# Expert jobs of 128 and of 64 slots in turn, and some weight low parts made by the Pool engine, in the expert stage of a two-layer decoder step

## The reference

```
def _swiglu(h, w_gate, w_up, w_down):
    return (jax.nn.silu(h @ w_gate) * (h @ w_up)) @ w_down

def _moe(h, w_router, b_router, w_gate, w_up, w_down):
    logits = (h @ w_router).astype(jnp.float32) + b_router.astype(jnp.float32)
    top_vals, top_idx = lax.top_k(logits, TOP_K)
    wts = jax.nn.softmax(top_vals, axis=-1)
    combine = jnp.sum(jax.nn.one_hot(top_idx, N_EXPERTS, dtype=jnp.float32) * wts[..., None], axis=-2)
    out = jnp.zeros_like(h)
    for e in range(N_EXPERTS):
        out = out + combine[..., e:e + 1] * _swiglu(h, w_gate[e], w_up[e], w_down[e])
    return out
```

## Time and profile before

| | us |
|---|---|
| median of 3 runs (lowest, highest) | 2112.4 (2107.23, 2112.99) |
| span of the profiled execution | 2107.7 |
| PE busy, share of the span | 2035.7, 97% |
| DVE busy | 1439.6, 68% |
| ACT busy | 1148.5, 54% |
| POOL busy | 130.5, 6% |
| DMA, mean rate over the span | 250 GB/s |

### The profile page before, as it was taken

The page is one execution under the profiler, slowest core; times in us unless marked ns, Lnnn a source line. Parts: engine busy times, 40 slices in busy tenths (PEclk is TensorE's granted clock), DMA queues, the critical chain, the costliest instruction groups (busy, mean ns, idle before and its releaser), DMA issues. The chain is left out here.

```text
span 2107.7 us, 34719 instructions
## 1 busy us (share of the span) xinstructions
PE 2035.7 (97%) x13413; PEld 1830.5 (87%) x13413; DVE 1439.6 (68%) x1595; ACT 1148.5 (54%) x1162; POOL 130.5 (6%) x170
## 2 busy tenths in 40 slices
PE   7999999999999999999999899999999999999997
PEld 5999999888999889989999688888888888888885
DVE  4477445555444455755454699898989898988987
ACT  4433334444333443432443568686868677776865
POOL 3100003200000030000230100000000000000000
PEclk9999999999999999999999999999999999999998
DMA  9634465654766454435654599999999999999996
GB/s 352 213 91 155 129 205 174 203 179 131 219 200 215 136 164 147 122 103 171 184 184 164 189 325 398 327 393 328 380 347 367 358 349 376 326 394 319 403 326 252
DMA packets 244081, 526.67 MB, mean 250 GB/s; under 512 B 18151, under 2 KB 142169, under 8 KB 243970
## 3 DMA queue, kind: packets, MB, share of 16 engines
q1 hardware_dynamic: 234304, 495.78, 67.0%
q0 software_dynamic: 9648, 29.29, 4.5%
q10 hardware_dynamic: 18, 0.04, 0.0%
HBM read 512.44 MB, written 12.59 MB: 249 GB/s over the span
## 5 line engine op out<-in xcount | busy, mean ns | idle before, releaser
L1688 ACT ACTIVATE mhi<-mraw 128x2048 fp32r<-128x2048 f32 (+1 forms) x318 | 574.0, 1819 | 210.5 <-DMA mraw<-in_w_exp_up 72.9
L1157 DVE TENSOR_TENSOR mlo<-mraw,mhi 128x2048 fp32r<-128x2048 f32 (+1 forms) x317 | 677.1, 2163 | 15.7 <-ACT mhi L1688 14.8
L571 DVE TENSOR_TENSOR wlo<-raw,whi 128x1024 fp32r<-128x1024 f32 x244 | 289.1, 1212 | 314.8 <-ACT whi L1397 313.6
L1973 PE MATMUL ps<-h1h,whi 128*128 128x320 f32 x1248 | 385.1, 321 | 8.8 <-DVE h1l L678 3.9
L1974 PE MATMUL ps<-h1l,whi 128*128 128x320 f32 x1248 | 370.7, 309 | 0.0
L2469 PE MATMUL ps<-mhi,xeh 128*128 128x512 f32 (+1 forms) x864 | 326.7, 378 | 1.8 <-DVE xel L1176 1.7
L2470 PE MATMUL ps<-mhi,xel 128*128 128x512 f32 (+1 forms) x864 | 321.3, 372 | 0.0
L1397 ACT ACTIVATE whi<-raw 128x1024 fp32r<-128x1024 f32 x244 | 247.8, 1046 | 118.9 <-PE ps L2358 44.9
L1973 PEld LDWEIGHTS ps<-h1h,whi 128*128 128x128 f32 x1248 | 235.3, 189 | 25.3 <-issue 18.7
L1974 PEld LDWEIGHTS ps<-h1l,whi 128*128 128x128 f32 x1248 | 235.5, 189 | 0.0
L2475 PE MATMUL ps<-mlo,xeh 128*128 128x512 f32 (+1 forms) x864 | 224.5, 371 | 0.0
(11 more groups left out here) (415 smaller groups left out, 2657.1 us busy)
## 6 DMA issues: line engine op xcount, KB each, us to landing
mraw<-in_w_exp_down SPq DMA_DIRECT2D x198, 512.0 KB, 8.6
mraw<-in_w_exp_gate SPq DMA_DIRECT2D x150, 512.0 KB, 5.5
mraw<-in_w_exp_up SPq DMA_DIRECT2D x144, 512.0 KB, 6.5
raw<-in_w_in SPq DMA_DIRECT2D x128, 512.0 KB, 3.9
raw<-in_w_ada SPq DMA_DIRECT2D x64, 512.0 KB, 3.8
mraw<-in_w_exp_gate SPq DMA_DIRECT2D x72, 384.0 KB, 3.6
mraw<-in_w_exp_up SPq DMA_DIRECT2D x72, 384.0 KB, 4.6
pause<-in_w_ada SPq DMA_DIRECT2D x32, 512.0 KB, 6.8
```

Source lines behind the costliest of these rows:

```text
L571: V.tensor_tensor(WLO[:, u % RAW_UNITS, 0:w], RAW[:, u % RAW_UNITS, 0:w], WHI[:, h % HI_UNITS, 0:w].bitcast(F32), ALU.subtract).then_inc(l ...
L1157: V.tensor_tensor(MLO[:, n % RAW_RING, 0:w], MRAW[:, n % RAW_RING, 0:w], MHI[:, n % HI_RING, 0:w].bitcast(F32), ALU.subtract).then_inc(m_l ...
L1688: A.activation(MHI[:, n % HI_RING, 0:w], MRAW[:, n % RAW_RING, 0:w], ACT.Copy).then_inc(m_hi, 1)
L1973: M.matmul(out_, w, v[0], start=start, stop=False, skip_group_check=True)
```

## The change

Only the expert stage changes, in three ways.

Jobs of 64 slots. Expert 0 stays job 0. The other seven are ranked by their number of tokens: the three largest become jobs 2, 4 and 6, the four smallest jobs 1, 3, 5 and 7. Jobs 0, 2, 4, 6 have 128 slots as before ("full" here), jobs 1, 3, 5, 7 have 64 ("half"), and so have extra jobs, of which there are up to six and each takes the next 64 tokens of an expert that has more than its slots. In a half job the stationary operand holds the 64 tokens' high parts in columns 0 to 63 and their low parts in columns 64 to 127 (`XEH`, and `GTH` in the down part), so lines 2470 and 2507 fall away: 8 matmuls a pair for 12. The halves of the result, in rows 0 to 63 and 64 to 127, are added in the `turn`: ACT copies the gate and up sums (`SG`, `SU`), TensorE multiplies each 128 x 128 block of both with `FOLD` (two unit matrices of 64 on each other) in place of one transpose, ACT takes the silu, DVE multiplies (`SGT`), and one pair later ACT and DVE split the product (`half_high`, `half_low`).

Pool makes the low parts of pairs 6, 11, 16, 21, 26 and 31 of jobs 0 to 6, and DVE leaves these out. Jobs 7 and later keep all 35 on DVE. Pool's fetch for the next job stands in its program between pair 16 and pair 21.

Order and tables. The ranking and the half jobs' tables make DVE's small table work in job 0 longer (nine pieces for five, from pair 2 on for pair 17), SP waits for `routed` after job 0's pairs and loads each job's expert number from `XI`, and job 7 has moved into the loop of extra jobs.

```diff
-EXTRA = 4
+HALF = 64
+MAIN = NE - 1
+EXTRA = 6
 JOBS = NE + EXTRA
+TURNS = 6
 HI_RING, RAW_RING = 5, 7
+POOL_PAIRS = (6, 11, 16, 21, 26, 31)
+DVE_PAIRS = PAIRS - len(POOL_PAIRS)
...
-TABLE_PAIRS = {17: 0, 20: 1, 22: 2, 25: 3, 28: 4}
+TABLE_PAIRS = {2: 0, 4: 1, 6: 2, 8: 3, 17: 4, 19: 5, 21: 6, 23: 7, 25: 8}
...
-            with sp.Fori(1, NE) as job:
-                load_job(job, job)
             sp.wait_ge(sem("routed"), 1)
-            extra = sp.value_load(XI[0:1, 4:5], min_val=0, max_val=EXTRA)
-            with sp.Fori(0, EXTRA) as k:
+            with sp.Fori(0, MAIN // 2) as two:
+                for job in (two * 2 + 1, two * 2 + 2):
+                    e = sp.value_load(XI[0:1, bass.ds(job, 1)], min_val=0, max_val=NE - 1)
+                    load_job(job, e)
+            extra = sp.value_load(XI[0:1, 15:16], min_val=1, max_val=1 + EXTRA)
+            with sp.Fori(0, 1 + EXTRA) as k:
                 with sp.If(k < extra):
-                    e = sp.value_load(XI[0:1, bass.ds(k, 1)], min_val=0, max_val=NE - 1)
-                    load_job(k + NE, e)
+                    e = sp.value_load(XI[0:1, bass.ds(k + MAIN, 1)], min_val=0, max_val=NE - 1)
+                    load_job(k + MAIN, e)
...
+                src, s = PS[:, FILL_BANKS[k], :].rearrange("p (k n) -> p k n", k=4), slice(4 * k, 4 * k + 4)
+                if half:
+                    V.tensor_tensor(XEH[:, s, HALF:P], src[:, :, HALF:P], XEH[:, s, 0:HALF].bitcast(F32),
+                                    ALU.subtract).then_inc(xe_out, 1)
+                else:
+                    V.tensor_tensor(XEL[:, s, :], src, XEH[:, s, :].bitcast(F32), ALU.subtract).then_inc(xe_out, 1)
...
+                (half_constants, ranks, main_slots, main_weights, blocks, owners, extra_slots, extra_weights,
+                 table_out)[part]()
+            def ranks():
+
+
+                n = [P, NE, NE]
+                st(V.tensor_tensor(OH[:, 0], KEY[:, 0:1, :].broadcast_to(n), KEY[:, 0, :].unsqueeze(2).broadcast_to(n),
+                                   ALU.is_gt))
+                st(V.tensor_reduce(KEY[:, 1, :], OH[:, 0], AX.X, ALU.add))
+                st(V.tensor_scalar(KEY[:, 2, :], KEY[:, 1, :], 3.5, None, ALU.is_gt))
+                st(V.tensor_scalar(KEY[:, 3, :], KEY[:, 2, :], 7.0, None, ALU.mult))
+                st(V.scalar_tensor_tensor(KEY[:, 3, :], KEY[:, 1, :], 2.0, KEY[:, 3, :], ALU.mult, ALU.subtract))
+                st(V.tensor_tensor(OH[:, 1], KEY[:, 3:4, :].broadcast_to(n),
+                                   CF[:, C_IOTA8:C_IOTA8 + NE].unsqueeze(2).broadcast_to(n), ALU.is_equal))
+
...
+            def half_low(job, number, k):
+
+
+                f0, nf = tile_at(k)
+                dve.wait_ge(gt_hi, job * TURNS + (k + 1))
+                V.tensor_tensor(GTH[:, f0:f0 + nf, HALF:P],
+                                SGT[:, k % 2, 0:nf * HALF].rearrange("p (k n) -> p k n", k=nf),
+                                GTH[:, f0:f0 + nf, 0:HALF].bitcast(F32), ALU.subtract).then_inc(half_lo, 1)
+
+            def job_dve(job, half, half_next, number=None, first=False, shared=True):
                 m_lo_part(job, 2)
...
                     if p == 0:
                         dve.wait_ge(sem("iw_made"), 1)
...
+                        for k in TURN_PAIRS[p - 1]:
+                            half_low(job, number, k)
                     for s, what, k in SIDE[p]:
...
+                                .then_inc(m_aux_out, 1)
+                        elif what == "turn" and half:
+                            n = tile_at(k)[1] * HALF
+                            dve.wait_ge(gate_out, job * TURNS + (k + 1))
+                            V.tensor_tensor(SGT[:, k % 2, 0:n], SGT[:, k % 2, 0:n], PS[:, bank, 256:256 + n], ALU.mult)\
...
-            with dve.Fori(1, NE) as job:
-                job_dve(job)
+            job_dve(0, False, True, first=True)
+            with dve.Fori(0, MAIN // 2) as two:
+                job_dve(two * 2 + 1, True, False, two)
+                job_dve(two * 2 + 2, False, True)
...
-            with dve.Fori(0, EXTRA) as k:
+            with dve.Fori(0, 1 + EXTRA) as k:
                 with dve.If(k < extra):
-                    job_dve(k + NE)
...
+            def half_high(job, k, s):
+
+
+                f0, nf = tile_at(k)
+                act.wait_ge(m_aux_out, job * JAUX + (AHEAD + s + 1))
+                A.activation(GTH[:, f0:f0 + nf, 0:HALF],
+                             SGT[:, k % 2, 0:nf * HALF].rearrange("p (k n) -> p k n", k=nf), ACT.Copy).then_inc(gt_hi, 1)
...
                 for p in range(PAIRS):
-                    if p < GPAIRS and p % KD == KD - 1:
+                    if half and p < GPAIRS and p % KD == KD - 1:
+                        g, w = p // KD, GROUPS[p // KD][1]
+                        for i in range(2):
+                            act.wait_ge(m_tile, job * 9 + (3 * g + 1 + 2 * i))
+                            A.activation(SG[:, i, 0:w], PS[:, GROUP_BANKS[g][2 * i], 0:w], ACT.Copy)
+                            if i == 0:
+                                act.wait_ge(m_tile, job * 9 + (3 * g + 2))
+                            else:
+                                act.wait_ge(m_used, job * PAIRS + (p + 1))
...
-                        if what == "turn":
+                        if what == "turn" and half:
+                            n = tile_at(k)[1] * HALF
+                            act.wait_ge(m_aux_in, job * JAUX + (s + 1))
+                            if k >= 2:
+                                act.wait_ge(half_lo, number * TURNS + (k - 1))
+                            A.activation(SGT[:, k % 2, 0:n], PS[:, 4 + s % 2, 0:n], ACT.Silu).then_inc(gate_out, 1)
+                        elif what == "turn":
...
+            def job_pool(job):
+
+                for i, n in enumerate(POOL_PAIRS):
+                    if i == len(POOL_PAIRS) // 2:
+                        gather(job + 1)
+                    w = 4 * GROUPS[n // KD][1] if n < GPAIRS else 2 * D
+                    pool.wait_ge(m_hi, job * PAIRS + (n + 1))
+                    pool.tensor_tensor(MLO[:, n % RAW_RING, 0:w], MRAW[:, n % RAW_RING, 0:w],
+                                       MHI[:, n % HI_RING, 0:w].bitcast(F32), ALU.subtract).then_inc(m_lo_pool, 1)
+
...
                 def lo_ready(p):
-                    pe.wait_ge(m_lo, job * PAIRS + (p + 1))
+                    if alone is not None:
+                        pe.wait_ge(m_lo, alone * PAIRS + (MAIN * DVE_PAIRS + p + 1))
+                    elif p in POOL_PAIRS:
+                        pe.wait_ge(m_lo_pool, job * len(POOL_PAIRS) + (POOL_PAIRS.index(p) + 1))
+                    else:
+                        pe.wait_ge(m_lo, job * DVE_PAIRS + (lows_ahead(p) + 1))
...
-                            M.matmul(o_, XEL[:, k, :], hi_[:, s], start=False, stop=False)
+                            if not half:
+                                M.matmul(o_, XEL[:, k, :], hi_[:, s], start=False, stop=False)
...
+                            if kf in TURNED and half:
+                                pe.wait_ge(half_lo, number * TURNS + (TURN_OF[kf] + 1))
+                            elif kf in TURNED:
...
-                            for m in range(tile_at(k)[1]):
+                            for m in range(tile_at(k)[1] if half else 0):
+                                for j, raw in enumerate((SG, SU)):
+                                    c0 = 256 * j + m * HALF
+                                    ins = M.matmul(PS[:, bank, c0:c0 + HALF], raw[:, k % 2, m * P:(m + 1) * P],
+                                                   FOLD[:, :], start=True, stop=True, skip_group_check=True)
```

More of the change, by code:

```diff
@@ L96, with lows_ahead @@
 TURNED = {tile_at(k)[0]: s for units in SIDE.values() for s, what, k in units if what == "turn"}
+def lows_ahead(n):
+    return n - sum(p < n for p in POOL_PAIRS)
+TURN_OF = {tile_at(k)[0]: k for k in range(TURNS)}
+TURN_PAIRS = {p: [k for _, what, k in units if what == "turn"] for p, units in SIDE.items()}
 PARTS = ["f", "q", "v", "i", "u", "g", "A", "ga", "gb", "B", "O"]
@@ L1266, in owners @@
                 ks = CF[:, C_IOTA8:C_IOTA8 + EXTRA].unsqueeze(2).broadcast_to(n)
[L1267 to L1271 removed]
+                own, shift = OH[:, 0, 0:EXTRA], OH[:, 1, 0:EXTRA]
@@ L1298, in job_dve @@
                 for p in range(PAIRS):
-                    if p < GPAIRS and p % KD == KD - 1:
+                    if not half and p < GPAIRS and p % KD == KD - 1:
                         w = GROUPS[p // KD][1]
@@ L1323, in job_dve @@
                     if p - 1 in FILLS:
-                        low_fill(FILLS[p - 1], job * 2 + (2 + FILLS[p - 1]))
+                        low_fill(FILLS[p - 1], job * 2 + (2 + FILLS[p - 1]), half_next)
+                    if half and p:
+                        for k in TURN_PAIRS[p - 1]:
+                            half_low(job, number, k)
                     for s, what, k in SIDE[p]:
@@ L1731, in job_act @@
```

(14 more changed lines are left out.)

187 lines of the change are left out of this document (114 added, 73 removed).

## The result

| | before | after |
|---|---|---|
| median of the runs, us (lowest, highest) | 2111.8 (2107.2, 2113.0; 4 runs with the one taken beside the change) | 2139.9 (2135.4, 2141.9; 4 runs) |
| ratio | | 1.0133, 95% interval 1.0116 to 1.0150 |
| span of the profiled execution, us | 2107.7 | 2140.1 |

The change made the kernel 28 us slower, where 25 us faster was forecast. The range given went to 2115, so the result lies outside it. It is near the rival on the slower side (2136).

The account below looks back on a forecast made before the run. TensorE was taken to set the time, transfers just behind. Job 0 at 101, jobs 1 to 6 at 576 and jobs 7 and 8 at 178.6 gave 855.6 for 881: span 2082, median 2087, range 2056 to 2115.

Parts of the forecast that it names:

- the rival on the slower side: DVE steps behind Pool's pairs, jobs 0 to 6: exclusion costs more than it gives; at 5 us an operation 2136; chance 0.14.
- What bounds the kernel: Expert stage: TensorE has no gap and sets the time, 97.9 us a job; transfers just behind, DVE 10 us behind them.
- the floor: Transfers of a job in the expert stage: 45.1, 18.6 and 28.1 us, together 91.8; no job can be shorter for long.
- the number of jobs: Expert stage: only the 170 tokens overflow, by 42, giving one extra job; nine jobs as before, with the same bytes.
- The price put on it: Clock in half jobs: TensorE idles a little, but the full clock was expected to be granted; costed at nothing.
- Pool's operations: Low parts on Pool: 4.0 us for 2048 columns and 3.0 for 1536, 22 us a job.
- The exclusion itself: Pool's and DVE's low parts: cannot run together; all of Pool's 22 us a job added to DVE's chain.
- The sum of DVE's chain: DVE's work plus Pool's 22 us: 96.7 us in a full job, 93.5 in a half job.
- the 2104: Time if Pool's operation takes the skill's 4.5 us at 2048 columns, making the chain some 2.5 us a job longer.
- 6 us of table work, partly hidden: Job 0: some 20 small table operations and waits add 6 us; DVE chain 105, part hidden, 101 taken.
- The free-Pool rival: Pool and DVE read side by side; transfers bound each two jobs at 183.6 us; 54 us less, 2059; chance 0.20.
- The 5 us of pairs ready: Jobs 7 and 8: pairs ready on ACT and DVE when a full job ends save some 5 us, giving 178.6.

Follow-up runs that it names:

- the fifth: Half jobs, all low parts on DVE, room for four extra jobs, plus six unread two-operand SBUF subtractions a job on Pool in jobs 0 to 6: 2192.7 us, ratio 1.0386.
- sixth runs: Half jobs, all low parts on DVE, room for four extra jobs, with three memsets on Pool at each of six places a job, reading nothing: 2088.7 us, ratio 0.9880.
- the last run: Changed kernel with room for four extra jobs and Pool's low parts only in jobs 1 to 6, DVE making all of job 0's: 2111.0 us, ratio 0.9997.
- the second run: Changed kernel with room for four extra jobs in place of six: 2126.0 us, ratio to the kernel before 1.0066.
- the first: Changed kernel with no low part on Pool, DVE making all 35 of every job: 2098.8 us, ratio to the kernel before 0.9929.
- the fourth: Changed kernel with all low parts on DVE and room for four extra jobs: 2088.6 us, ratio to the kernel before 0.9888.
- the seventh run: Changed kernel with all low parts on DVE, room for six extra jobs, and Pool fetching tokens only for jobs that are run: 2082.1 us, ratio 0.9857.

## Why the prediction was wrong, point by point

Three of its steps failed: the length of Pool's operation, the overlap taken for job 0, and the end, which was left out. The forecast had a span of 2082 and the profiled one was 2140.1. The 58 us between them are: job 0 +11.5 (112.5 for 101), jobs 1 to 6 +25.2 (601.2 for 576), jobs 7 and 8 +7.3 (185.9 for 178.6), the end +10.2 and the start +4.8 (with rounding, 59).

**What bounds the kernel, the floor, the number of jobs.** Right. Nine jobs were run. Where nothing but a half job's own work counts, jobs 7 and 8 of all the runs with half jobs, it took 91.6 to 95.5 us; the second of two half jobs in a row took 91.6 to 92.5 against the 91.8 worked out from the earlier trace rows.

**TensorE.** Right within what can be read: full jobs 97.0 to 97.8 us (once 99.0) without Pool, and TensorE busy for some 80 of 92 us in job 8, with 74 expected (the busy time holds more than the distances between starts). The clock did fall at times in half jobs: 0.91 in the mean of job 1 of after, 0.98 in job 8, where nothing was lost that can be seen. The price put on it, nothing, fits jobs of 92 us, but no run separates it. ACT and DVE came out as worked out where Pool has no part: in jobs 7 and 8 of after ACT was busy for 73 to 74 us (under 80) and DVE for 84.2 and 85.1 (84.0).

**Pool's operations: the term that was mis-sized.** 4.0 and 3.0 us had been taken by scaling a row of 512 columns. Undisturbed they last 4.56 and 3.47 us (the shortest of the 28 and of the 14 of after), and with the wait for DVE's operation in front 5.40 and 4.07 in the mean. Per job this is 30 us for 22, 5.0 us an operation. Here the Trainium skill ("GPSIMD Engine Reference", section 3.1) had the better figure, 4.5 us; the prediction named it and kept its own. The exclusion itself was forecast rightly, and the fifth and sixth runs show it, and that it is for reading: low parts of up to 6.4 us beside reads, none over 2.34 us beside fills of the same length. That is the rule of the Trainium skill, "SBUF — State Buffer", section "Who interferes with whom": a GpSimd instruction that only writes does not contend with a DVE instruction with two SBUF inputs.

**The sum of DVE's chain.** The prediction said that at 4.3 us an operation the gain is gone and that 5 us give 2136 with two-job chains of 206 us. The operations were 5 us, the time 2140, but the two-job chains only 199.8 to 201.4. That rival's working was 5 to 6 us a chain too long, and not of the right kind. It added Pool's whole time to DVE's (30 us a job), of which 12 to 15 us show as waiting in DVE's records, and it took DVE for full, which idled for 13 us a job. What the trace shows instead is late results, DVE's and Pool's own, in front of TensorE; the sign that the rival named, TensorE waiting for Pool's low parts, is there with 9.1 us in jobs 1 to 6. That the total came near the rival's is chance: the end, the start, jobs 7 and 8 and the 112.5 us of job 0 (108 in that rival) filled the gap. One sum of the prediction is off by itself, the 2104 for 2.5 us more a job: the chain of a full and a half job would then be 195.2 us, where 192 had been taken, and the time some 2099.

**Job 0.** 101 was taken, between 98 and 105; it was 112.5. The step that failed is "6 us of table work, partly hidden". The tables cost nothing (99.2 us with them, without Pool). The cost is Pool's operations beside them: 14 us, by the last run.

**The end.** Left out altogether. `EXTRA` from 4 to 6 was read as room in a table. It adds two fetches to the end of Pool's queue, 10 us, which the second run took back. The step that failed is the one that costs a moved or added operation on every queue: Pool's program was read up to the last job and not to its end.

**The free-Pool rival and the hand-overs.** Its premise fell, and its number would have been too low as well: with Pool out of it altogether and the end of before, the kernel took 2088.6, not 2059. Without Pool's operations (the first, the fourth and the seventh run) a full and a half job take 189.5 to 192.4 us together, not the 183.6 of the transfers alone, and half jobs behind a full one 92.4 to 95.5. The 5 us of pairs ready at the end of a full job were never seen. In a full job the transfers run at TensorE's pace (a share of 0.96); that they have no more than a few pairs ready when it ends would explain this, but is not shown. Why a half job behind a full one is 1 to 4 us longer than one behind a half is open.

**The range.** With the cases as given it left out 0.18 on the slow side; the case that came had been given 0.14.

## What to carry to other kernels

Work moved from DVE to Pool relieves DVE only if the two can run together; if both read SBUF, DVE with two operands, each waits for the other's whole operation, and here the waiting (13.3 us a job) took back what was saved (12.6), with late results on top. A sum of busy times does not show the last part: DVE was no busier than before. A record's duration contains the wait for the other engine, so compare an operation's time beside and away from the other engine before calling an engine busy. And when a constant is raised that stands for "room", read every queue to its last instruction: work for cases that don't occur may end the kernel.

## What the runs showed of the hardware that was not expected

- Pool's reading and DVE's low parts did not run side by side: each of the 32 and 31 that began inside the other's in after lasted the other's rest and its own time, to within 0.14 us. Six added operations of 4 us a job, whose result nobody reads, made each full job behind job 0 10.6 to 12.6 us longer (107.6 to 109.6 for 97.0), though DVE had 10 us of room in it, and fills of the same length made it 0.0 to 0.8 longer.
- The same subtraction of 2048 columns takes Pool 4.56 us undisturbed and DVE 2.28.
- At the end of the kernel a fetch by an indirect transfer from Pool (128 rows of 4 KB) is 0.94 us of Pool and lets the next start 4.3 to 5.8 us after its own start; ahead of the last of these gaps in after, 4.3 us, no other transfer had been issued for 6.2 us.
